# x laid out turned by the host, its norm put on the products, in the input projection of a one-core encoder block

## The chip, the core and the metric

One core of a Trainium2 chip runs the whole block in one launch. The metric is the device time of that launch in microseconds (us). TensorE (PE) multiplies, VectorE (DVE), ScalarE (ACT) and GpSimd (POOL) work on the rest, and transfers are issued on SyncE's queue (SP), on ACT's or on POOL's.

## The reference

The block takes x, 1024 rows of 1024 values in fp32, and computes

```python
h = rms_norm(x, norm1_g[l])
proj = h @ w_in[l]
xr, gr, q, k, v, fl = jnp.split(proj, cuts, axis=-1)
xr = causal_depthwise_conv(xr, conv_w[l], conv_b[l])
y_lru = rg_lru(xr, ...)
y_lru = y_lru * jax.nn.gelu(gr)
log_f = jax.nn.log_sigmoid(fl + fox_bf[l])
y_fox = forgetting_attention(q, k, v, log_f)
x = x + concat(rms_norm(y_lru), rms_norm(y_fox)) @ w_out[l]
x = x + peer(rms_norm(x), ...)
return rms_norm(x, final_g)
```

rms_norm multiplies a row by 1/sqrt(mean of its squares + 1e-6) and each column by a gain. That first factor, one number per row, is called the row root here. Only rms_norm(x, norm1_g) and its product with w_in (1024 x 2568: xr, gr, q, k and v of 512 columns each, fl of 8) are touched by the change. Everything after that product is computed as before.

## The kernel before, in words

The kernel is five stages, one behind the other, each a block of its own that begins when all engines have ended the one before: project (L114), recur (L358), attend (L612), the mixing with w_out, and the expert stages, which hold most of the time. The change is in project and recur.

**The operand.** The product needs h with its columns on the partitions. It lies in m.hh, 8 slices k of 128 columns times 1024 rows, and twice: a high part that ACT rounds and a low part, what is left, that DVE subtracts. The weights of 128 columns of w_in (a chunk i, 20 in all) are split the same way into m.w_hi and m.w_lo. m.w, m.w_hi and m.w_lo hold two chunks each. A product of a chunk for 512 rows (a half) is three terms of 8 matmuls 128x512 (three_terms, L102 to L111): high by high, high by low, low by high. So a product is 24 matmuls.

**project before.** SP loads x in 8 blocks of 128 rows into a ring of four (L164), with the gain on all partitions (L166) and the weights of chunks 0 and 1 (L92). For each block, ACT squares and sums the rows (L214) and takes the root (L216), DVE inverts it (L275) and multiplies row root and gain onto the block (L278, normalize), PE turns the block in 8 transposes (L312, turn), ACT rounds what it reads from PSUM (L208, high) and DVE subtracts (L261, low; one input in PSUM). A product of half 0 needs blocks 0 to 3, one of half 1 all 8. The order is written out by hand: items (L152) begins with chunks 0 and 1 for half 0, then both for half 1, and the last turns lie between and inside the first two products. Then come chunks 2 to 6, the 8 forget columns (L338), and chunk 7. ACT reads every product from PSUM and writes it where it is kept (L247, with gelu for chunks 4 to 7; L242 and L243 for the forget columns). Four PSUM banks hold products in flight. In the same loop ACT rounds the weights of chunk i + 2 (L99) and DVE subtracts (L266). POOL only zeroes tiles and then loads the forget weights, the biases and small constants in a chain of transfers (L180 to L188), each waited for.

**recur before.** It holds 12 chunks, 8 to 19: q, k and v of four pairs of heads. PE multiplies them and in between makes the gates of the recurrence (gates_of, L456 to L465) and turns v (turn_v, L467). ACT reads the products (L495), rounds weights (L99), and makes the sigmoids, tanh, exp and root of one of four channel groups c (L518 to L530). POOL subtracts for the weights' low parts (L443), one 128x1024 operation of two SBUF inputs per chunk, in place of DVE. DVE runs, in order: conv(0), the logarithm of the forget gate, and then for each c fraction(c), conv(c + 1), recurrence(c). PE's gates wait for conv. The sigmoids of c + 1 wait for recurrence(c), because they overwrite r and i (lru_done, L513), and the second pair of gate products of c + 1 needs the two gate banks that those sigmoids read.

## Time and profile before

| what | us |
|---|---|
| three runs, median (lowest to highest) | 2739.32 (2738.11 to 2740.86) |
| profiled execution | 2739.89 |
| its span in the trace | 2738.1 |
| project, from the start to the restart of PE in recur | 0 to 126.8 |
| recur | 126.8 to 279.0 |
| attend, mixing and experts | 279.0 to 2738.1 |

Busy over the span: PE 2669.0 us (97%), DVE 2325.6 (85%), POOL 1443.5 (53%), ACT 1272.2 (46%). A busy share is a mean over stages of very different kinds. For this change one reads the first 280 us by themselves: when PE starts, when it does not run, and what it waits for there.

### The profile page before, as it was taken

The page shows a single profiled execution, that of the slowest core. Times are in us where ns is not written, and L with a number is a line of the kernel's source. Part 1 is how long each engine was busy: PE and PEld are TensorE (multiplying, and loading weights), DVE is VectorE, ACT ScalarE, POOL GpSimd, SP SyncE. Part 2 cuts the span into 40 slices and gives each one's busy share as a digit, 9 for nine tenths or more (in the row PEclk, how much of TensorE's full clock was granted, in tenths as well). Part 3 has the DMA queues.
Part 4 walks back from the last instruction along what each step waited for, and adds up shares of the span by engine and source line. Part 5 has one row for each costly group of instructions (what it writes and reads, how often), then busy time and mean ns, then how long its engine had stood idle before and what let it go on. Part 6 is the DMA issues. An engine that isn't in the chain of part 4 may idle for free. (4 is left out here: it accounts for less than half of the span.)

```text
span 2738.1 us, 40138 instructions
## 1 busy us (share of the span) xinstructions
PE 2669.0 (97%) x14907; PEld 2363.1 (86%) x14907; DVE 2325.6 (85%) x4160; ACT 1272.2 (46%) x2553; POOL 1443.5 (53%) x938
## 2 busy tenths in 40 slices
PE   7999899989999999999999999999999999999998
PEld 6777566679999999999999999997888888888887
DVE  4287897449989999988889898877999999999997
ACT  4244443223332223999898998962222222222222
POOL 2122321024348876666666666654666666666652
PEclk9999899999999999999999999999999999999999
DMA  4110101233248886999999999999999999999995
GB/s 128 39 39 24 62 1 39 77 100 101 62 159 304 304 295 223 376 393 399 398 389 410 402 389 405 394 393 371 388 387 387 387 388 388 388 386 388 388 386 207
DMA packets 333059, 762.67 MB, mean 279 GB/s; under 512 B 24176, under 2 KB 159344, under 8 KB 330304
## 3 DMA queue, kind: packets, MB, share of 16 engines
q0 software_dynamic: 111104, 403.02, 38.8%
q1 hardware_dynamic: 221040, 353.68, 36.1%
q10 hardware_dynamic: 720, 3.41, 0.3%
q8 instruction: 118, 1.93, 0.3%
q14 instruction: 77, 0.63, 0.1%
HBM read 667.73 MB, written 92.27 MB: 278 GB/s over the span
## 5 line engine op out<-in xcount | busy, mean ns | idle before, releaser
L2159 POOL DMA_INDIRECT v_rows<-in_peer_v,row_numbers x336 | 542.0, 1613 | 322.7 <-DVE y_rest L2232 184.7
L1790 PE MATMUL expert_pre<-h2T,wq_then_uT_hi 128*128 128x320 f32 x4096 | 669.3, 312 | 2.3 <-PEq L1469 2.3
L1904 POOL DMA_INDIRECT u_rows<-in_peer_u,row_numbers x384 | 534.9, 1393 | 241.5 <-DVE row_weights L1924 163.3
L1790 PEld LDWEIGHTS expert_pre<-h2T,wq_then_uT_hi 128*128 128x128 f32 x4096 | 609.4, 188 | 2.4 <-issue 2.4
L2289 PE MATMUL expert_out<-v_hi,w_hi 128*128 128x512 f32 x1280 | 500.4, 391 | 11.7 <-DVE w_lo L2210 10.3
L1924 DVE CUSTOM_DVE_ANT_0 u_rows<-u_rows,h_rows_kept 128x1024 f32<-128x1024 f32 x384 | 489.1, 1301 | 23.9 <-DMA u_rows<-in_peer_u,row_numbers 23.6
L2289 PE MATMUL expert_out<-v_lo,w_hi 128*128 128x512 f32 x1280 | 498.8, 390 | 0.0
L2289 PE MATMUL expert_out<-v_hi,w_lo 128*128 128x512 f32 x1280 | 498.7, 390 | 0.0
L1790 PE MATMUL expert_pre<-h2T,wq_then_uT_lo 128*128 128x320 f32 x2048 | 342.0, 309 | 0.0
L2232 DVE SCALAR_TENSOR_TENSOR y_rest<-v_rows,row_weights,y_rest 128x1024 f32<-128x1024 f32 x256 | 326.8, 1280 | 17.9 <-DMA v_rows<-in_peer_v,row_numbers 17.2
L1790 PEld LDWEIGHTS expert_pre<-h2T,wq_then_uT_lo 128*128 128x128 f32 x2048 | 310.9, 188 | 0.0
L2289 PEld LDWEIGHTS expert_out<-v_hi,w_hi 128*128 128x128 f32 x1280 | 240.8, 188 | 66.4 <-DVE w_lo L2210 14.6
L2179 ACT ACTIVATE w_hi<-pick_memory 128x640 fp32r<-128x640 f32 x128 | 94.6, 739 | 436.8 <-DVE pick_memory L2203 436.8
L2289 PEld LDWEIGHTS expert_out<-v_hi,w_lo 128*128 128x128 f32 x1280 | 240.7, 188 | 50.3
L2289 PEld LDWEIGHTS expert_out<-v_lo,w_hi 128*128 128x128 f32 x1280 | 240.9, 188 | 49.6
L1856 ACT ACTIVATE gated_second_hot<-gated_second_hot,routeT,minus_second_and_gate 128x128 f32<-128x128 f32 x640 | 262.9, 485 | 0.2
L2177 ACT ACTIVATE v_hi<-pick_memory 128x1024 fp32r<-128x1024 f32 x128 | 134.9, 1054 | 197.2 <-DMA pick_memory<-in_peer_v 139.3
L1838 ACT ACTIVATE expert_acts<-expert_pre 128x320 f32<-128x320 f32 x256 | 110.0, 430 | 238.0 <-PE expert_pre L1790 237.4
L1848 ACT ACTIVATE gated_second_hot<-iota,minus_second_and_gate 128x128 f32<-128x128 f32 x640 | 203.4, 393 | 0.0
L2216 DVE TENSOR_TENSOR v_lo<-pick_memory,v_hi 128x1024 fp32r<-128x1024 f32 x128 | 156.1, 1219 | 18.2 <-ACT v_hi L2177 18.2
L1778 PE MATMUL spread_ps<-gated_second_hot,first_hot 128*128 128x128 f32 x1280 | 168.3, 274 | 0.0
L110 PE MATMUL product<-hT_hi_lo,w_in_hi 128*128 128x512 f32 x640 | 159.1, 402 | 5.4 <-PEq L158 3.2
(351 smaller groups left out, 3996.2 us busy)
## 6 DMA issues: line engine op xcount, KB each, us to landing
pick_memory<-in_peer_v SPq DMA_DIRECT2D x128, 512.0 KB, 11.7
wq_then_u<-in_peer_u_turned SPq DMA_DIRECT2D x86, 512.0 KB, 8.3
pick_memory<-acts_dram SPq DMA_DIRECT2D x128, 320.0 KB, 11.3
acts_dram<-expert_acts SPq DMA_DIRECT2D x124, 320.0 KB, 6.0
gates_dram<-pick_memory SPq DMA_DIRECT2D x19, 2048.0 KB, 11.1
pick_memory<-gates_dram SPq DMA_DIRECT2D x58, 448.0 KB, 13.0
third_u<-in_peer_u_turned SPq DMA_DIRECT2D x42, 512.0 KB, 8.5
wq_then_u<-in_peer_wq SPq DMA_DIRECT2D x32, 512.0 KB, 3.9
```

The lines of the kernel that those rows point to most:

```text
L110: last = nc.tensor.matmul(to, w[:, i % 2, k], m.hh[:, part, k, cols], start=n == 0, stop=n == len(terms) - 1)
L1778: last = nc.tensor.matmul(spread_ps[:, g % 2, j], first_hot[:, g % SLOTS, j], second[:, g % SLOTS, j], start=True, stop=True)
L1790: last = nc.tensor.matmul(pre[:, (2 * c + half) % 4, 0:WIDTH], part[:, c % 2, k], m.h2T[:, t, k, HALVES[half]], start=n == 0, stop=n == le ...
L1848: last = A(second[:, g % SLOTS, j], m.iota[:], ACT.Abs, bias=minus[:, i % 2, 0, first + j:first + j + 1])
L1856: last = A(second[:, g % SLOTS, j], second[:, g % SLOTS, j], ACT.Relu, scale=minus[:, i % 2, 1, first + j:first + j + 1], bias=routeT[:, i ...
L1904: pool.indirect_dma_start(rows[:, k % RING], None, table, bass.IndirectOffsetOnAxis(ap=m.row_of[:, f, slot:slot + 1], axis=0)).then_inc(fe ...
L1924: v.tensor_tensor_reduce(out=rows[:, k % RING], in0=rows[:, k % RING], in1=m.h2_kept[:, f], scale=1.0, scalar=0.0, op0=ALU.mult, op1=ALU.a ...
L2159: pool.indirect_dma_start(rows[:, k % ROW_RING], None, d.peer_v, bass.IndirectOffsetOnAxis(ap=m.row_of[:, f, slot:slot + 1], axis=0)).then ...
L2177: nc.scalar.activation(vhi[:, n % 2, c], vt[x % V_RING], ACT.Copy).then_inc(vhi_done, 1)
L2216: v.tensor_tensor(vlo[:, n % 2, c], vt[x % V_RING], vhi[:, n % 2, c].bitcast(F32), ALU.subtract).then_inc(vlo_done, 1)
L2232: v.scalar_tensor_tensor(out=m.y_of(f), in0=rows[:, k % ROW_RING], scalar=m.row_weight[:, f, slot:slot + 1], in1=m.y_of(f), op0=ALU.mult, ...
L2289: last = nc.tensor.matmul(out[:, bank], a[:, n % 2, c, tokens], e[:, n % 2, c, cols], start=opens and c == 0 and k == 0, stop=closes and c ...
```

## The change

The host hands in x turned (columns first, x_turned) beside x, and the gain as 128x8. In project, SP loads x_turned in 8 slices k of 128 columns by 1024 rows; all eight have room. The slices are split without the norm: ACT multiplies by the gain while it rounds (high), and DVE makes the low part in one operation from xT and the high part (low, both inputs in SBUF). ACT also squares every slice, and POOL adds the eight squares, 7 additions of 128x1024. PE sums them over the partitions with a matrix of ones (sum_squares, placed behind the fifth product). DVE and ACT make the row root of that, on all partitions (m.root, 128x1024), and it is multiplied onto the products: by DVE in project, as it reads them from PSUM (evict), by POOL in recur, on q, k and v after ACT has stored them, and by DVE on the last v.

PE's first four products (chunks 0 and 1, both halves, four banks) are made slice by slice: three terms of slice k for chunk 0, then for chunk 1, up to k = 3; then slices 4 to 7 for chunk 0, and for chunk 1. The transposes are gone. There are six PSUM banks for products. The first weights come in two parts, the first halves issued by ACT. The forget columns get root and bias in three DVE operations behind the last eviction. In recur, POOL scales 11 chunks, and turn_v waits for that; the convolutions write into parts of xrT that are done with. Between the code that is quoted lie the semaphores' new counts, memory and the host's arrays.

```diff
 def split_high(act, nc, m, i):
-
-    act.wait_ge(m.w_in[i % 2], 16 * (i // 2 + 1))
+    act.wait_ge(m.w_in[i % 2], 16 * (i // 2 + 2))
...
-        items = [(0, 0), (1, 0), (0, 1), (1, 1)] + [(i, half) for i in [*range(2, CHUNKS - 1), FORGET, CHUNKS - 1]
-                                                    for half in range(2)]
+        items = [(i, half) for i in [*range(CHUNKS - 1), FORGET, CHUNKS - 1] for half in range(2)]
...
             def _(sp):
+                def load_x(k):
+                    if k >= X_RING:
+                        sp.wait_ge(x_in[k % X_RING], 16 * (k // X_RING))
+                    sp.dma_start(xT[:, k], d.x_turned[k * P:(k + 1) * P, :]).then_inc(x_in[k % X_RING], 16)
+
+                for k in range(X_RING):
+                    load_x(k)
+                for k in range(X_RING, KT):
+                    if k - X_RING < 2:
+                        sp.wait_ge(m.w_in[k - X_RING], 16)
+                        load_weights(sp, d, m, k - X_RING, PARTS[1])
+                    load_x(k)
...
             def _(pool):
+                for k in range(1, KT):
+                    pool.wait_ge(squared, k + 1)
+                    if k > 1:
+                        pool.wait_ge(zeroed_then_added, BLOCKS + k - 1)
+                    pool.tensor_tensor(square_sum[:], squares[:, 0] if k == 1 else square_sum[:], squares[:, k % SQ_RING],
+                                       ALU.add).then_inc(zeroed_then_added, 1)
                 pool.dma_start(wf[:], d.w_in[:, 5 * G:].rearrange("(k p) n -> p k n", p=P)).then_inc(small_in, 16)
...
+                def high(k):
+                    act.wait_ge(x_in[k % X_RING], 16 * (k // X_RING + 1))
+                    A(m.hh[:, 0, k], xT[:, k], ACT.Copy, scale=gain[:, k:k + 1]).then_inc(high_done, 1)
+
+                def square(k):
+                    if k >= SQ_RING:
+                        act.wait_ge(zeroed_then_added, BLOCKS + max(1, k - SQ_RING))
+                    A(squares[:, k % SQ_RING], xT[:, k], ACT.Square).then_inc(squared, 1)
...
+                act.dma_start(gain[:], d.norm1_turned).then_inc(gain_in, 16)
+                for i in range(2):
+                    load_weights(act, d, m, i, PARTS[0])
...
+                split_part(0, 0)
+                act.wait_ge(gain_in, 16)
+                for k in range(KT):
+                    if k == 1:
+                        split_part(1, 0)
+                    high(k)
+                    if k:
+                        square(k - 1)
+                    if k in (3, 4):
+                        split_part(k - 3, 1)
+                square(KT - 1)
+                for i in range(2):
+                    act.wait_ge(product_done, used(i))
+                    split_high(act, nc, m, i + 2)
+                for half in range(2):
+                    act.wait_ge(mean_made, half + 1)
+                    A(m.root[:, cols_of(half)], m.root[:, cols_of(half)], ACT.Sqrt).then_inc(rooted, 1)
...
+                    if half == 1 and i >= 2:
                         act.wait_ge(product_done, used(i))
                         split_high(act, nc, m, i + 2)
+                    if i >= CT:
+                        act.wait_ge(product_read, reads(n))
+                        gate = m.gateT[:, i - CT, cols_of(half)]
+                        A(gate, gate, ACT.Gelu_apprx_tanh)
...
+                def low(k):
+                    dve.wait_ge(high_done, k + 1)
+                    v.scalar_tensor_tensor(out=m.hh[:, 1, k], in0=xT[:, k], scalar=gain[:, k:k + 1],
+                                           in1=m.hh[:, 0, k].bitcast(F32), op0=ALU.mult, op1=ALU.subtract
+                                           ).then_inc(low_done, 1)
...
+                def evict(n):
+                    i, half = items[n]
+                    dve.wait_ge(product_done, n + 1)
+                    g, c = divmod(i, CT)
+                    to, pad = (m.xrT, d.PAD) if g == 0 else (m.gateT, 0)
+                    v.tensor_tensor(to[:, c, pad + half * HALF:pad + (half + 1) * HALF], product[:, n % BANKS],
+                                    m.root[:, cols_of(half)], ALU.mult).then_inc(product_read, 1)
...
+                split_low(0, PARTS[0], 1)
+                for k in range(KT):
+                    low(k)
+                    if k == 0:
+                        split_low(1, PARTS[0], 2)
+                    if k in (3, 4):
+                        split_low(k - 3, PARTS[1], k)
+                split_low(2)
+                split_low(3)
+                mean(0)
+                mean(1)
+                invert(0)
+                evict(0)
+                invert(1)
...
+                    if half == 1 and i >= 2:
+                        split_low(i + 2)
+                    if i == CHUNKS - 1:
+                        dve.wait_ge(rooted, 2 + half + 1)
+                        part = m.forget[:, cols_of(half)]
+                        own.link(v.tensor_tensor(part, part, forget_more[:, cols_of(half)], ALU.add))
+                        own.link(v.tensor_tensor(part, part, m.root[0:d.FH, cols_of(half)], ALU.mult))
+                        v.tensor_scalar(part, part, fbias[:], None, ALU.add)
...
+                def first_products(i, k):
+                    if k in (0, KT // 2):
+                        pe.wait_ge(m.w_hi_done, i + 1 + (2 if k else 0))
+                    pe.wait_ge(high_done, k + 1)
+                    for term, (w, part) in enumerate(((m.w_hi, 0), (m.w_hi, 1), (m.w_lo, 0))):
+                        if term == 1:
+                            pe.wait_ge(low_done, k + 1)
+                        if term == 2 and k in (0, KT // 2):
+                            pe.wait_ge(m.w_lo_done, i + 1 + (2 if k else 0))
+                        for half in range(2):
+                            end = k == KT - 1 and term == 2
+                            last = nc.tensor.matmul(product[:, 2 * i + half], w[:, i, k], m.hh[:, part, k, cols_of(half)],
+                                                    start=k == 0 and term == 0, stop=end)
...
+                def sum_squares():
+                    pe.wait_ge(zeroed_then_added, BLOCKS + KT - 1)
+                    for half in range(2):
+                        nc.tensor.matmul(sums[:, half], ones[:], square_sum[:, cols_of(half)], start=True, stop=True
+                                         ).then_inc(summed, 1)
+
+                for k in range(KT // 2):
+                    for i in range(2):
+                        first_products(i, k)
+                for i in range(2):
+                    for k in range(KT // 2, KT):
+                        first_products(i, k)
+                for n in range(4, len(items)):
...
+                    if n == 4:
+                        sum_squares()
...
-                for i in range(FIRST + 2, CHUNKS):
-                    pool.wait_ge(m.w_hi_done, i + 1)
-                    pool.tensor_tensor(m.w_lo[:, i % 2], m.w[:, i % 2], m.w_hi[:, i % 2].bitcast(F32), ALU.subtract
-                                       ).then_inc(low_done, 1)
+                for i in range(FIRST, CHUNKS - 1):
+                    pool.wait_ge(product_read, 2 * (i - FIRST) + 2)
+                    p, which = divmod(i - FIRST, 3)
+                    to = (m.q[:, p], m.k[:, p], vT(p))[which]
+                    pool.tensor_tensor(to, to, m.root[:], ALU.mult).then_inc(scaled, 1)
+                    if i + 2 < CHUNKS:
+                        pool.wait_ge(m.w_hi_done, split_count(i + 2))
+                        pool.tensor_tensor(m.w_lo[:, i % 2], m.w[:, i % 2], m.w_hi[:, i % 2].bitcast(F32), ALU.subtract
+                                           ).then_inc(low_done, 1)
+                pool.wait_ge(scaled, CHUNKS - 1 - FIRST)
...
                 def turn_v(p):
-                    pe.wait_ge(product_read, 6 * p + 6)
+                    pe.wait_ge(scaled, 3 * p + 3)
...
                 dve.wait_ge(lru_done, CT)
+                for half in range(2):
+                    n, cols = 2 * (CHUNKS - 1 - FIRST) + half, slice(half * HALF, (half + 1) * HALF)
+                    dve.wait_ge(product_done, n + 1)
+                    v.tensor_tensor(vT(PAIRS - 1)[:, cols], product[:, n % 4], m.root[:, cols], ALU.mult)
...
+        if name == "x":
+            turned = _np.ascontiguousarray(a.T)
```

## Rows read from the trace of the kernel before

**Rows 1.** Busy time by stage: stretch, length, each engine's busy us, clock, DMA.
```profile
0.00:22.08 22.08, 7.85 (x33) 6.28 (x33) 9.90 (x17) 11.73 (x20) 2.23 (x11) 1.00 0.79 261
22.08:39.80 17.72, 16.61 (x81) 13.52 (x81) 13.12 (x19) 9.78 (x19) 5.13 (x7) 1.00 0.31 63
...
124.00:262.00 138.00, 133.66 (x562) 104.55 (x563) 108.89 (x74) 66.41 (x82) 41.08 (x24) 0.99 0.14 39
```

**Rows 2.** Timeline (start, us, engine, line, tiles, idle before), PE's products in project.
```profile
22.08 5.55 PE L110 MATMUL product<-hT_hi_lo,w_in_hi 128*128 128x512 f32 x16 [1.11 <-ACT hT_hi_lo L208]
50.80 3.79 PE L110 MATMUL product<-hT_hi_lo,w_in_hi 128*128 128x512 f32 x16
```

**Rows 3.** Timeline of the first x blocks, and transfers up to 130 us.
```profile
5.83 1.06 ACT L214 ACTIVATE squares<-x_rows 128x1024 f32<-128x1024 f32 x1 [2.31 <-DMA x_rows<-in_x]
...
w_in_columns<-in_w_in SPq DMA_DIRECT2D x12, 512.0 KB, 4.2
```

**Rows 4.** Timeline and groups by shape: the operations that the change multiplies.
```profile
8.35 1.29 DVE L278 SCALAR_TENSOR_TENSOR h_rows<-x_rows,sums,gain 128x1024 f32<-128x1024 f32 x1
...
21.92 1.05 ACT L214 ACTIVATE squares<-x_rows 128x1024 f32<-128x1024 f32 x1
...
L722 POOL TENSOR_TENSOR squares_summed<-squares_summed,squares_T 128x1024 f32<-128x1024 f32 x5 | 11.9, 2376 | 18.0 <-ACT squares_T L890 17.7
```

**Rows 5.** Timeline of DVE and POOL where both have two-input work, mixing and recur.
```profile
140.63 6.54 DVE L78 RECIPROCAL qT<-qT 8x1024 f32<-8x1024 f32 x1
141.36 2.40 POOL L443 TENSOR_TENSOR w_in_lo<-w_in_columns,w_in_hi 128x1024 fp32r<-128x1024 f32 x1 [1.48 <-ACT w_in_hi L99]
165.09 2.28 DVE L601 TENSOR_TENSOR_SCAN forget<-qT 8x1024 f32<-8x1024 f32 x1
166.59 3.62 POOL L443 TENSOR_TENSOR w_in_lo<-w_in_columns,w_in_hi 128x1024 fp32r<-128x1024 f32 x1 [7.72 <-ACT w_in_hi L99]
...
176.56 5.95 DVE L564 SCALAR_TENSOR_TENSOR x_conv<-x_proj_then_attention,conv_taps,x_conv 128x1024 f32<-128x1024 f32 x3
178.36 3.06 POOL L443 TENSOR_TENSOR w_in_lo<-w_in_columns,w_in_hi 128x1024 fp32r<-128x1024 f32 x1 [8.15 <-ACT w_in_hi L99]
236.11 3.93 DVE L564 SCALAR_TENSOR_TENSOR x_conv<-x_proj_then_attention,conv_taps,x_conv 128x1024 f32<-128x1024 f32 x3
...
470.61 2.89 POOL L1094 TENSOR_TENSOR w_out_fox_lo<-w_out_fox_then_x_rows,w_out_fox_hi 128x1024 fp32r<-128x1024 f32 x1 [39.44 <-ACT w_out_fox_hi L1137]
471.21 2.84 DVE L1165 TENSOR_TENSOR fox_columns_lo<-x_proj_then_attention,fox_columns_hi 128x512 fp32r<-128x512 f32 x1
473.45 1.50 POOL L1099 CAST wq_then_uT_hi<-wq_then_u 128x1024 fp32r<-128x1024 f32 x1
481.29 0.69 DVE L1165 TENSOR_TENSOR fox_columns_lo<-x_proj_then_attention,fox_columns_hi 128x512 fp32r<-128x512 f32 x1
```

**Rows 6.** Timeline: project's end and recur's start; a reciprocal (by shape).
```profile
110.42 0.68 DVE L302 TENSOR_TENSOR forget<-forget,forget_of_low_weights 8x512 f32<-8x512 f32 x1 [2.22 <-ACT forget_of_low_weights L243]
...
125.30 1.23 DVE L266 TENSOR_TENSOR w_in_lo<-w_in_columns,w_in_hi 128x1024 fp32r<-128x1024 f32 x1 [10.49 <-ACT w_in_hi L99]
...
126.85 5.50 PE L110 MATMUL product<-hT_hi_lo,w_in_hi 128*128 128x512 f32 x16 [3.17 <-PEq L158]
...
L999 DVE RECIPROCAL inverse_totals<-mixed_values 64x512 f32<-64x512 f32 x16 | 53.7, 3355 | 10.4 <-PE mixed_values L824 10.1
```

**Rows 7.** Timeline of recur: the recurrence, the sigmoids that wait, and PE's gates.
```profile
187.26 1.23 DVE L588 TENSOR_TENSOR gateT<-gateT,i_gate 128x1024 f32<-128x1024 f32 x1
190.47 1.27 ACT L518 ACTIVATE r_gate<-gates,lru_vectors 128x512 f32<-128x512 f32 x2
194.63 1.88 PE L464 MATMUL gates<-x_conv,wx_blocks 128*128 128x512 f32 x4
198.44 0.69 DVE L575 TENSOR_SCALAR x_proj_then_attention<-tanh_m 128x1024 f32<-128x1024 f32 x1 [9.96 <-ACT tanh_m L524]
...
222.01 1.26 ACT L518 ACTIVATE r_gate<-gates,lru_vectors 128x512 f32<-128x512 f32 x2 [5.34 <-DVE gateT L588]
222.75 1.98 PE L464 MATMUL gates<-x_conv,wx_blocks 128*128 128x512 f32 x4 [1.31 <-ACT r_gate L518]
```

More of the change, by code:

```diff
@@ L218, in _ @@
+                for i in range(2):
+                    load_weights(act, d, m, i, PARTS[0])
                 act.wait_ge(m.ident_ready, 2)
                 A(first_root[:], m.ident[:, 0:1], ACT.Sqrt)
-                for b in range(X_RING):
-                    root(b)
-                    if b:
-                        high(b - 1)
-                split_high(act, nc, m, 0)
-                high(X_RING - 1)
-                root(X_RING)
-                split_high(act, nc, m, 1)
-                root(X_RING + 1)
@@ L229, in _ @@
-                high(X_RING)
-                for b in range(X_RING + 2, NT):
-                    root(b)
-                    high(b - 1)
-                high(NT - 1)
+                split_part(0, 0)
[8 more added lines that the diff above has]
+                        split_part(k - 3, 1)
@@ L238, in _ @@
+                A(wf_hi, wf[:], ACT.Copy).then_inc(forget_split, 1)
                 for n, (i, half) in enumerate(items):
-                    act.wait_ge(product_done, n + 1)
                     if i == FORGET:
-                        cols = slice(half * HALF, (half + 1) * HALF)
-                        A(m.forget[:, cols], product[0:d.FH, n % 4], ACT.Identity, bias=fbias[:])
-                        A(forget_more[:, cols], product[LOW:LOW + d.FH, n % 4], ACT.Copy).then_inc(product_read, 1)
+                        act.wait_ge(product_done, n + 1)
+                        A(m.forget[:, cols_of(half)], product[0:d.FH, n % BANKS], ACT.Copy)
+                        A(forget_more[:, cols_of(half)], product[LOW:LOW + d.FH, n % BANKS], ACT.Copy
+                          ).then_inc(rooted, 1)
@@ new lines, in split_low, with mean @@
+                def split_low(i, rows=slice(None), count=None):
+                    dve.wait_ge(m.w_hi_done, count or split_count(i))
+                    v.tensor_tensor(m.w_lo[:, i % 2, rows], m.w[:, i % 2, rows], m.w_hi[:, i % 2, rows].bitcast(F32),
+                                    ALU.subtract).then_inc(m.w_lo_done, 1)
+                def mean(half):
+                    dve.wait_ge(summed, half + 1)
+                    v.tensor_scalar(m.root[:, cols_of(half)], sums[:, half], 1.0 / D, EPS, ALU.mult, ALU.add
+                                    ).then_inc(mean_made, 1)
@@ new lines, in invert @@
+                def invert(half):
+                    dve.wait_ge(rooted, half + 1)
+                    own.link(v.reciprocal(m.root[:, cols_of(half)], m.root[:, cols_of(half)]))
+                def evict(n):
[5 more added lines that the diff above has]
+                                    m.root[:, cols_of(half)], ALU.mult).then_inc(product_read, 1)
@@ L296, in _ @@
-                v.tensor_tensor(wf_lo, wf[:], wf_hi.bitcast(F32), ALU.subtract).then_inc(forget_lo, 1)
-                for i in range(2, CHUNKS + 1):
-                    split_low(i)
-                for half in range(2):
-                    dve.wait_ge(product_read, items.index((FORGET, half)) + 1)
-                    part = m.forget[:, half * HALF:(half + 1) * HALF]
-                    v.tensor_tensor(part, part, forget_more[:, half * HALF:(half + 1) * HALF], ALU.add)
-                split_low(CHUNKS + 1)
+                split_low(0, PARTS[0], 1)
@@ L332, in multiply_forget, with multiply @@
+                def multiply(n):
+                    i, half = items[n]
+                    if half == 0:
+                        pe.wait_ge(m.w_hi_done, split_count(i))
+                        pe.wait_ge(m.w_lo_done, split_count(i))
+                    if n >= BANKS:
+                        pe.wait_ge(product_read, n - BANKS + 1)
+                    three_terms(nc, m, product[:, n % BANKS], i, half).then_inc(product_done, 1)
                 def multiply_forget(n):
-                    cols = slice(items[n][1] * HALF, (items[n][1] + 1) * HALF)
@@ L540, in _ @@
                     for n, (chunk, half) in enumerate((c, h) for c in range(i, i + 3) for h in range(2)):
-                        evict(chunk, half)
+                        if chunk < CHUNKS - 1:
+                            evict(chunk, half)
                         if n == 0 and p:
```

193 lines of the change are left out of this document (69 added, 124 removed).

## The prediction

> **What bounds the kernel now.** I read the busy time by stage first. PE is busy for 7.9 of the first 22.1 us and for 16.6 of the next 17.7; from there to the end of project it has no gap, and in recur it is busy for 133.7 of 138 us [rows 1]. So a saving has to come from the first 40 us, and in the long stretch behind them DVE and ACT are idle most of the time. The timeline of PE comes second. The first product begins at 22.08 and the fifth at 50.80 [rows 2], so the first four end at about 50.7. Two spacings follow: 16 matmuls take 3.6 to 3.8 us at full pace (a product of 24 takes 5.44), and the first 16 took 5.55 [rows 2]. I take the difference, 1.6 us or more, as what PE pays when it starts slow. [...] It pays again at 126.85, behind 3.2 us of idleness, with 5.50 us for 16 [rows 6]. Third, the timeline of DVE and POOL where both have something to do, because the change gives POOL 18 operations of 128x1024 with two SBUF inputs (7 additions, 11 scalings) that it did not have.
>
> **POOL and DVE, the price that decides.** A three-operation run of DVE takes 3.93 us alone and 5.95 us when a POOL subtraction falls into it, and that one takes 3.06 in place of 2.40 [rows 5]. The row pair at 470 us shows who goes first: POOL starts at 470.61 and waits half a us for DVE's operation to end, then DVE's 0.69 us operation takes 2.84, then POOL's copy waits for DVE in turn (1.50 us) [rows 5]. So they alternate, one operation each. A reciprocal is not held (6.54 us, with POOL's 2.40 inside it) [rows 5]. Once POOL waited over two, a scan and the operation behind it (3.62) [rows 5]; that is the only sign against alternation. [...]
>
> **Start of project after.** x slice 0 lands as block 0 does (ACT starts at 5.83 [rows 3]). The half weights come on ACT's queue, which before does not show; 512 KB of them take 4.2 us undisturbed [rows 3], so from 2.6 us on they land at 5.5 at the soonest and about 8 in the crowd. I take 6.8; both ends shift the start by about 1 us. ACT then has 8 highs, 8 squares and 4 half splits, at 1.05 us recorded and 0.95 apart for 1024 elements [rows 4]: high(0) ends at 8.4, high(1) 9.8, squares 0 and 1 by 12.7, high(3) 13.6, high(4) 16.0, high(5) 18.4, high(6) 20.3, high(7) 22.1. ACT never waits for low, and a slice lands before it is wanted. The first addition can start at 12.7. low costs 1.29 (the two-input form [rows 4]), an addition 2.38 [rows 4]. low(0) to low(2) are done by 13.0. From there five lows and two half splits (0.65 each) alternate with seven additions, because squares come each 1.9 to 2.4 us, faster than the pair of operations goes by: low(3) ends at 16.7, low(4) 23.5, low(5) 30.2, low(6) 33.9, the last addition 36.3, low(7) 37.6. The sum is 7 x 2.4 + 5 x 1.29 + 2 x 0.65 = 24.6 behind 13.0.
>
> PE begins at 8.4, is through slices 0 to 3 for both chunks at 20.6 (8 shares of 6 matmuls, 1.36 us each, the start slow), and then waits: for low(4) 2.4 us, low(5) 5.3, low(6) and low(7) each 1 to 3 us, with the pace down. Behind 37.6 come four slow matmuls (1.7 us) and 24 for chunk 1 (5.44 and about 0.8 slow): the fourth product ends at 45.5 where it ended at 50.7. **Gain 5.2.** Unhindered, it would have ended at 31.9 (24 x 4 matmuls in 21.8 us, and the slow start), a gain of 18.8.
>
> **Rest of project.** sum_squares adds two fp32 matmuls to PE's queue. A pair of that form, the gates, takes 1.88 recorded, 1.8 of PE's time [rows 7]: **+1.8**. The root's chain (mean, sqrt, a reciprocal of 512 at 3.36 [rows 6], an eviction of 0.69) is 6 us behind the first sum, and the seventh product, which wants bank 0, comes 6.3 us behind it: 0.5 us to spare, nothing if that holds, up to 1 us if not. Evictions on DVE (16 of 0.69, one SBUF input) and the gelus on ACT lie beside products of 5.44. POOL's chain of constants starts at 36 in place of 22.8 and needs 47 us: it ends near 84, covered by project's end. At the end, DVE's split for chunk 9 (1.23, before at 125.30 [rows 6]) can start 0.5 earlier, since ACT reads no product first; but three forget operations (0.68, 0.68, 0.4 and gaps, [rows 6]) come behind it: **+1.35** until recur starts. The last gelu is covered by them.
>
> **recur.** POOL scales chunk i when ACT has stored it, and then subtracts for chunk i + 2. Its own load is 4.8 us of 10.9 per chunk, up to 9 when DVE holds it: it meets PE's needs, and turn_v's. What counts is DVE. Each scaling costs it 2.0 to 2.3 us unless it meets a reciprocal [rows 5]. By the clock of before, scalings start at 140.3 (beside a reciprocal, free), 154.7, 165.6, 177.3 and 188.2. The second to fourth delay conv(1) by 5.7 us, to 188.1, so PE's first gates wait 0.9 us. The fifth and the subtraction behind it, which before began at 189.24 just behind recurrence(0), both fall into recurrence(0), 4.6 us more: it ends at 198.8, where it ended at 188.5 [rows 7]. The sigmoids of channel group 1 ran at 190.47 and could have run 2.0 earlier for DVE's part; their first half now ends at 199.5, and PE's second gates, at 194.6 before [rows 7], wait for it: 5.1 us with the 0.9, and 1.6 for the slow pace behind the idleness. DVE's idleness at 198.44 (9.96 us [rows 7]) pays the debt off. For group 2 the sigmoids already waited 5.34 us for recurrence(1), and PE 1.31 for them [rows 7]: two more POOL operations meet that recurrence and add 2.1 net. For group 3 the sigmoids come 2.5 us late, and PE's gates, four us behind them in the timeline, do not wait. Sum **+8.5 to +10**; I take 8.5, as the 1.6 may be partly in rows already. The last v on DVE costs 0.1. Bounds: 0 if everything hides, 11 with a second slow start.
>
> **The sum** against the profiled 2739.9: -5.2 + 1.8 + 1.35 + 8.5 = +6.5, so 2746.4; the median of the runs lies 0.6 below that execution, so 2746. All behind recur starts from its end and is taken to shift with it, within 2 us.
>
> **Rivals.** (1) *DVE keeps its turn.* Its operations in project are not linked by waits of its own, and if DVE takes two or three in a row before POOL, as with the scan at 165 [rows 5], low(7) ends by 25 and the fourth product at 32: gain 18 to 18.8, less 3.2 in project; in recur 3 to 8.5 lost. That is 2728 to 2732, I say **2730**, faster; it decides from low(5) ending before 23. Against it: the pair at 470 is the same form (a satisfied wait, then the operation) and POOL got in. Chance 0.2. (2) *Recur absorbs it.* Project as forecast (-2.05), and DVE loses less than 6 us up to the end of recurrence(0): PE then hardly waits, -2.05 + 0 to 2 = **2738 to 2740**. For: several scalings begin within a us of a reciprocal or of DVE idleness, and POOL may slip into it. Chance 0.2. (3) *PE's clock is lost more often*, with an eviction late on top: two more slow starts, 3.2, and 1 to 3 for the seventh product: **2752**. Chance 0.1. That x arrives so late that it sets the pace, so that the slices do nothing, would need a slice landing behind 22; all of x had landed by 22 before, with 0.5 MB more in front. It goes with the forecast.
>
> **How the numbers follow.** Forecast, alternation in both stages: chance 0.5, by itself 2742 to 2751. About 0.2% (5.5 us, 2733.8 to 2744.8) is what can be told from no change. The range 2730 to 2752 takes in rival 1 to its middle and the other two; a tenth is left below, and under a tenth above. Three quarters of the forecast's chance lie above 2744.8. Slower: 0.5 x 0.75 + 0.1 = 0.48. Same: 0.5 x 0.25 + 0.2 = 0.32. Faster: 0.2.
>
> **What would show it.** In the changed kernel's timeline: low(4) to low(7) with recorded durations of 3 us or more, each started before a POOL addition ends, and PE idle for hT_hi_lo between 20 and 38 us; the fifth product at 45 to 46; recur's restart near 124; the sigmoids of group 1 waiting some 8 us for gateT, and PE for them. If lows take 1.3 each and low(7) ends by 25, the alternation is wrong and rival 1 holds. If recur is as long as before (152 us from restart to attend), rival 2.

## The result and the profile after

The changed kernel takes 2746.61 us (median of 8 runs, 2741.65 to 2749.44), the kernel before 2739.70 on the same chip (8 runs). The ratio is 1.0025, with a 95% interval of 1.0016 to 1.0035: slower by a quarter of a percent. The forecast was 2746. Its profiled execution took 2745.85 us, with a span of 2744.1; that of before has a span of 2738.1.

The stages, in us of each profiled span (recur is counted from PE's first product in it to the first transfer of attend):

| | before | after | forecast for after |
|---|---|---|---|
| PE's first product begins | 22.08 | 12.28 | 8.4 |
| fifth product begins | 50.80 | 45.77 | 45.5 |
| recur begins | 126.85 | 124.83 | 124.8 |
| attend begins | 279.04 | 287.49 | 285.5 |
| recur's length | 152.2 | 162.7 | 160.7 |
| end of the span | 2738.1 | 2744.1 | 2744.6 |

The busy time of the changed kernel by stage (stretch, length, busy us of PE, PE's weight loads, DVE, ACT and POOL, the TensorE clock that was granted as a share of the full one, DMA share, GB/s) answers to [rows 1]:

```profile
0.00:45.55 45.55, 25.85 (x96) 19.34 (x97) 27.88 (x14) 20.66 (x23) 26.13 (x23) 0.96 0.46 147
45.55:124.80 79.25, 74.81 (x326) 58.06 (x324) 30.59 (x34) 17.08 (x23) 8.48 (x14) 1.00 0.17 39
124.80:287.50 162.70, 154.59 (x632) 119.52 (x632) 138.95 (x80) 68.44 (x83) 72.85 (x35) 0.96 0.12 33
```

PE does 96 matmuls in the first 45.55 us, 25.9 us of work. In recur DVE's 80 operations take 139 us, and PE's clock is granted at 0.96 where it was 0.99 in [rows 1].

The start of the changed kernel, from its timeline (start, us, engine, line, tiles, idle time before and what ended it); [rows 2] and [rows 3] are its counterparts:

```profile
10.46 0.63 ACT L228 ACTIVATE w_in_hi<-w_in_columns 128x512 fp32r<-128x512 f32 x1 [5.45 <-DMA w_in_columns<-in_w_in]
...
12.28 2.45 PE L350 MATMUL product<-hT_hi_lo,w_in_hi 128*128 128x512 f32 x4 [12.28 <-ACT hT_hi_lo L219]
...
16.71 2.55 POOL L189 TENSOR_TENSOR ares_of_row_by_partition<-squares 128x1024 f32<-128x1024 f32 x1 [13.25 <-ACT squares L224]
...
17.70 2.64 DVE L278 SCALAR_TENSOR_TENSOR hT_hi_lo<-xT,gain,hT_hi_lo 128x1024 fp32r<-128x1024 f32 x1 [0.71 <-ACT hT_hi_lo L219]
...
19.41 18.74 POOL L189 TENSOR_TENSOR ares_of_row_by_partition<-ares_of_row_by_partition,squares 128x1024 f32<-128x1024 f32 x6
...
20.27 2.90 DVE L284 TENSOR_TENSOR w_in_lo<-w_in_columns,w_in_hi 128x512 fp32r<-128x512 f32 x1
...
23.09 3.43 DVE L278 SCALAR_TENSOR_TENSOR hT_hi_lo<-xT,gain,hT_hi_lo 128x1024 fp32r<-128x1024 f32 x1
...
26.45 2.88 DVE L284 TENSOR_TENSOR w_in_lo<-w_in_columns,w_in_hi 128x512 fp32r<-128x512 f32 x1
...
29.25 9.99 DVE L278 SCALAR_TENSOR_TENSOR hT_hi_lo<-xT,gain,hT_hi_lo 128x1024 fp32r<-128x1024 f32 x3
...
32.66 1.22 PE L350 MATMUL product<-hT_hi_lo,w_in_hi 128*128 128x512 f32 x2 [4.43 <-DVE hT_hi_lo L278]
...
39.29 0.73 PE L350 MATMUL product<-hT_hi_lo,w_in_hi 128*128 128x512 f32 x2 [1.65 <-DVE hT_hi_lo L278]
...
45.77 3.79 PE L111 MATMUL product<-hT_hi_lo,w_in_hi 128*128 128x512 f32 x16
```

The reader is to see three things. The half weights, 256 KB a chunk on ACT's queue, are there only at 10.46. From the first addition (16.71) on, seven operations of DVE, five lows and two half splits, take 21.84 us where alone they are 5 of 1.28 and 2 of 0.69, 7.8 in all: DVE is held for 14.0 us, 2.0 for each of the seven additions. And PE waits four times for a low: 0.93, 4.43, 0.38 and 1.65 us, 7.4 in sum.

The middle of recur answers to [rows 7], again from the timeline:

```profile
178.90 2.77 DVE L609 TENSOR_SCALAR x_proj_then_attention<-x_proj_then_attention,conv_taps,lru_vectors 128x1024 f32<-128x1024 f32 x1
...
186.26 2.75 POOL L484 TENSOR_TENSOR kT<-kT,w_root_on_all_partitions 128x1024 f32<-128x1024 f32 x1 [5.14 <-ACT kT L540]
186.80 3.29 DVE L633 TENSOR_TENSOR x_conv<-x_conv,tanh_m 128x1024 f32<-128x1024 f32 x1
188.97 3.37 POOL L487 TENSOR_TENSOR w_in_lo<-w_in_columns,w_in_hi 128x1024 fp32r<-128x1024 f32 x1
190.13 4.37 DVE L634 TENSOR_TENSOR_SCAN i_gate<-r_gate,x_conv 128x1024 f32<-128x1024 f32 x1
194.53 1.23 DVE L636 TENSOR_TENSOR gateT<-gateT,i_gate 128x1024 f32<-128x1024 f32 x1
195.79 1.26 ACT L563 ACTIVATE r_gate<-gates,lru_vectors 128x512 f32<-128x512 f32 x2 [7.36 <-DVE gateT L636]
```

A scaling holds the product in front of the scan (3.29 us), and the subtraction behind it holds the scan (4.37). The first row is of another kind: a tensor_scalar in fp32 with one SBUF input, 2.77 us where the same operation takes 0.81 at 210.70; POOL subtracts beside it, from 177.74 for 3.38 us. recurrence(0) ends 70.9 us behind recur's start; before it ended 61.6 behind it [rows 7]. ACT's sigmoids of group 1, which had waited for nothing, wait 7.36 us, and PE waits for them. PE's own timeline shows the cost, twice:

```profile
196.53 3.65 PE L509 MATMUL gates<-x_proj_then_attention,wx_blocks 128*128 128x512 f32 x4 [3.37 <-ACT r_gate L563]
...
228.46 3.78 PE L509 MATMUL gates<-x_proj_then_attention,wx_blocks 128*128 128x512 f32 x4 [3.38 <-ACT r_gate L563]
231.26 5.55 PE L111 MATMUL product<-hT_hi_lo,w_in_hi 128*128 128x512 f32 x16
```

Each wait is 3.4 us, and each pair of gates behind it takes 3.65 or 3.78 us where it took 1.88 and 1.98 [rows 7]. At 231.26 the next 16 matmuls are slow too, 5.55 us where such a row has 4.2 to 4.5 behind the other gates. The stretch by itself, in the busy times:

```profile
224.83:234.83 10.00, 6.62 (x15) 3.75 (x14) 3.47 (x3) 4.93 (x7) 0.00 (x0) 0.66 0.20 52
```

The mean granted clock is 0.66, so PE spent a part of it at the lower of its two levels, 1.2 GHz for 2.4.

### The profile page after: what moved, and what is told of

The parts are those of the page before. It is cut to its first block and busy times, and to the rows that moved or that the text cites. A ratio compares the mean times of both kernels' runs of the same rounds, so it can differ in the third digit from the quotient of the medians.

```text
span 2744.1 us, 39997 instructions
## 1 busy us (share of the span) xinstructions
PE 2664.7 (97%) x14847; PEld 2356.2 (86%) x14847; DVE 2369.2 (86%) x4164; ACT 1266.9 (46%) x2531; POOL 1487.6 (54%) x957
## 5 line engine op out<-in xcount | busy, mean ns | idle before, releaser
L2341 PE MATMUL expert_out<-v_hi,w_hi 128*128 128x512 f32 x1280 | 500.3, 391 | 10.6 <-DVE w_lo L2262 10.5
L1830 PEld LDWEIGHTS spread_ps<-gated_second_hot,first_hot 128*128 128x128 f32 x1280 | 160.8, 191 | 0.0
```

Of the source, the lines that this page charges most:

```text
L1830: last = nc.tensor.matmul(spread_ps[:, g % 2, j], first_hot[:, g % SLOTS, j], second[:, g % SLOTS, j], start=True, stop=True)
L2341: last = nc.tensor.matmul(out[:, bank], a[:, n % 2, c, tokens], e[:, n % 2, c, cols], start=opens and c == 0 and k == 0, stop=closes and c ...
```

## The experiments

The two places where POOL meets DVE were taken away first, one at a time and both. All ratios are to the kernel before, in runs on the same chip.

**e1_adds8: seven additions of 8 columns.** The sum of squares is right in 8 columns of 1024; the others hold a constant.

```diff
-pool.tensor_tensor(square_sum[:], ..., squares[:, k % SQ_RING], ALU.add)
+few = slice(0, 8)
+pool.tensor_tensor(square_sum[:, few], ..., squares[:, k % SQ_RING, few], ALU.add)
```

> The changed kernel, but POOL's seven additions of the squares are 8 columns wide instead of 1024 (the other 1016 columns of the sum are a constant), so the row root is not that of x; every wait stays. Theory (DVE and POOL exclude each other while both read two SBUF operands): the low parts take 1.3 us each instead of 3.0 to 3.4, the fourth product ends at about 35.6 us instead of 45.6 (31.9 of the unhindered walk plus the 3.7 us by which ACT started late), and the run is about 10 us shorter than the changed kernel, near 2736.6. Rival (ACT's pace or the arrival of x sets PE's waits between 25 and 40 us, the long low parts are only in step with it): the fourth product stays at 45 and the time near 2746.

2738.75 us (10 runs), ratio 0.9995, 0.9985 to 1.0004. The timeline of DVE, POOL and PE:

```profile
20.34 1.28 DVE L279 SCALAR_TENSOR_TENSOR hT_hi_lo<-xT,gain,hT_hi_lo 128x1024 fp32r<-128x1024 f32 x1 [0.35 <-ACT hT_hi_lo L220]
...
26.84 1.29 DVE L279 SCALAR_TENSOR_TENSOR hT_hi_lo<-xT,gain,hT_hi_lo 128x1024 fp32r<-128x1024 f32 x1 [0.71 <-ACT hT_hi_lo L220]
...
36.84 3.79 PE L111 MATMUL product<-hT_hi_lo,w_in_hi 128*128 128x512 f32 x16
```

The lows take 1.28 or 1.29 and end 11.1 us earlier, and the fifth product begins at 36.84 in place of 45.77, recur at 115.9. So the additions cost 8.9 us at this place, and nothing else there held PE. The fifth product is 1.2 us later than I had expected, the time 2.2 above it.

**e2_scale8: scalings of 8 columns.** q, k and v of recur are scaled by the row root in 8 of 1024 rows.

```diff
-pool.tensor_tensor(to, to, m.root[:], ALU.mult).then_inc(scaled, 1)
+pool.tensor_tensor(to[:, 0:8], to[:, 0:8], m.root[:, 0:8], ALU.mult).then_inc(scaled, 1)
```

> The changed kernel, but POOL's eleven scalings of q, k and v are 8 columns wide, so q, k and v keep their values without the row root; every wait stays. Theory (exclusion, read by way of DVE's chain): recurrence(0) ends about 4.6 us earlier relative to recur's start plus 5.7 us of what came before it, PE no longer waits 3.4 us twice for the sigmoids, recur takes 152 to 153 us instead of 162.7, and the run is about 10 us shorter, near 2736.6. Rival (what costs is the changed order of the convolutions, with their buffers in xrT, and their new wait): recur stays within 2 us of 162.7.

2736.54 us (10 runs), ratio 0.9988, 0.9978 to 0.9997. The row of recur in the busy times by stage:

```profile
124.79:276.92 152.13, 149.59 (x632) 117.54 (x632) 120.14 (x80) 68.56 (x83) 47.88 (x35) 0.99 0.13 35
```

Recur is 152.1 us long, as before (152.2). DVE's 80 operations take 120.1 us, 18.8 less than beside the 11 full scalings, 1.7 us for each.

**e3_both8: both edits.**

> Both narrowings at once; the computation left out is that of the two kernels before it. Theory: the two costs are in different stages, so they add: about 20 us shorter than the changed kernel, near 2726, 13 us below the kernel before. Rival (what is saved in front is given back later, since the expert stages are bound by transfers and indirect loads): less than 15 us of the 20 arrive at the end.

2728.11 us (4 runs), ratio 0.9954, 0.9939 to 0.9969. Fifth product at 37.57, recur from 116.64 to 269.42. Of the changed kernel's 2746.6 the additions take 7.9 us, the scalings 10.1, both together 18.5. (The changed kernel was timed beside 2739.7 for the kernel before and these three beside 2740.3, so each may be 0.6 more.) The rest of the change is therefore worth 12 us (2728.1 beside 2740.3 for the kernel before), and the 18 POOL operations eat more than that.

**e4_sum_on_pe: no POOL additions.** The whole computation; ACT writes the squares rounded for TensorE (fp32r), and PE sums them over partitions and slices in 16 matmuls between its first products.

```diff
-for k in range(1, KT): pool.tensor_tensor(square_sum[:], ..., squares[:, k % SQ_RING], ALU.add)
+def sum_squares(k):
+    pe.wait_ge(squared, k + 1)
+    for half in range(2):
+        nc.tensor.matmul(sums[:, half], ones[:], squares[:, k % SQ_RING, cols_of(half)], start=k == 0,
+                         stop=k == KT - 1).then_inc(summed, 1)
```

> Full computation. No additions on POOL: ACT writes the squares rounded for TensorE, and PE sums them slice by slice with 16 matmuls by the ones matrix, accumulated in PSUM, laid between the first products. Theory: as with the narrow additions the low parts are free, at the price of 16 matmuls of 0.227 us (3.6 us) in place of the two fp32 ones (1.8 us): the fifth product begins near 39 us instead of 45.6, and the run is about 8 us shorter than the changed kernel, near 2738.5, so within 0.2% of the kernel before. Rival (ACT's pace): near 2746.

2739.16 us (11 runs), ratio 1.0002, 0.9993 to 1.0011. PE's timeline:

```profile
13.05 2.45 PE L343 MATMUL product<-hT_hi_lo,w_in_hi 128*128 128x512 f32 x4 [13.05 <-ACT hT_hi_lo L212]
...
21.44 0.63 PE L370 MATMUL square_sums_of_rows<-squares,ones_square 128*128 128x512 f32 x2
21.91 1.08 PE L343 MATMUL product<-hT_hi_lo,w_in_hi 128*128 128x512 f32 x4
...
41.65 3.79 PE L111 MATMUL product<-hT_hi_lo,w_in_hi 128*128 128x512 f32 x16
```

PE has no gap from 13.05 on. A pair of summing matmuls takes 0.47 us of its time, eight of them 3.7; with a start 0.65 us later than e1's, that is 4.4 of the 4.8 us by which the fifth product comes later than in e1. I had expected it near 39, 2.65 us earlier: e1's fifth product was itself 1.2 us later than expected, PE started 0.65 later still, and the slow first matmuls took 0.3 more than in e1. The summing I had priced nearly right, at 3.6. Recur begins at 118.91, 5.9 us before after's: 4.1 from the start and 1.8 from the two fp32 matmuls that are gone.

**e5_memset_for_scale: POOL busy, but reading nothing.** In place of each scaling, three fills of m.root, which take 2.98 us. q, k and v of recur stay unscaled.

```diff
-pool.tensor_tensor(to, to, m.root[:], ALU.mult).then_inc(scaled, 1)
+for part in range(3):
+    pool.memset(m.root[:], 1.0).then_inc(scaled, 1)
+    pool.wait_ge(scaled, 3 * (i - FIRST) + part + 1)
```

> The changed kernel, but each of POOL's eleven scalings is three fills of m.root with 1.0 (128x1024, about 0.9 us each, so 2.7 us and nothing read), so q, k and v are not multiplied by the row root; POOL is as busy as with the scalings, its subtractions start as late, and turn_v waits as long. Theory A (what excludes DVE's two-input operations is POOL's reading of SBUF): recur is as short as with the narrow scalings, 152 to 154 us, the run near 2736.6. Theory B (any POOL operation on SBUF holds DVE, as the 5.2 us fill at recur's start holds a tensor_scalar), or what costs is that POOL's low weights and scaled v come late: recur stays at 160 or more and the run near 2745.

2737.93 us (10 runs), ratio 0.9995, 0.9986 to 1.0005. Recur is 152.3 us long. The timeline of POOL and DVE beside one set of fills and the subtraction behind it:

```profile
212.68 2.98 POOL L485 MEMSET w_root_on_all_partitions<- 128x1024 f32 x3 [2.88 <-ACT qT L542]
213.37 1.23 DVE L635 TENSOR_TENSOR x_proj_then_attention<-x_proj_then_attention,tanh_m 128x1024 f32<-128x1024 f32 x1
214.63 2.29 DVE L636 TENSOR_TENSOR_SCAN i_gate<-r_gate,x_proj_then_attention 128x1024 f32<-128x1024 f32 x1
215.74 3.37 POOL L489 TENSOR_TENSOR w_in_lo<-w_in_columns,w_in_hi 128x1024 fp32r<-128x1024 f32 x1
216.95 3.23 DVE L638 TENSOR_TENSOR gateT<-gateT,i_gate 128x1024 f32<-128x1024 f32 x1
```

The product and the scan run at their 1.23 and 2.29 us beside the fills; the subtraction, which reads SBUF, waits for the scan and then holds the next product (3.23). It is POOL's reading that holds DVE's operations of two SBUF inputs, not POOL's being busy, nor the waits and semaphores of the scalings, which are all still there. The Trainium skill (SBUF — State Buffer, "Who interferes with whom") says so too: a DVE instruction with two SBUF inputs contends with a GpSimd instruction that reads SBUF, and not with one that only writes it. This run shows it for such operations alone: the tensor_scalar at recur's start, with one SBUF input, takes 5.72 us here beside POOL's fill of 5.22, where a later one of its size takes 0.82.

**e6_one_queue: the first half weights in SP's queue, each ahead of its x slice.** The whole computation.

```diff
                 for k in range(X_RING):
+                    if k < 2:
+                        load_weights(sp, d, m, k, PARTS[0])
                     load_x(k)
...
-                for i in range(2):
-                    load_weights(act, d, m, i, PARTS[0])
```

> Full computation. The changed kernel, but SP issues the first halves of the two weight chunks in front of x slices 0 and 1; ACT's queue carries the gain alone. Theory: the weights, in 512-byte rows on a queue of their own, landed behind 2 MB of x in 4096-byte rows (10.46 us, 8 us after their issue); in one queue they land at 6 to 7, ACT's first high part ends near 8.5 instead of 12.1, the low parts' alternation with POOL begins 3.5 us earlier, and the run is 3 us shorter than the changed kernel, near 2743.5. Rival (the alternation or the sum has slack at its front): no difference, 2746.5.

2743.14 us (11 runs), ratio 1.0015, 1.0006 to 1.0024. The timeline of ACT and PE:

```profile
5.19 0.63 ACT L230 ACTIVATE w_in_hi<-w_in_columns 128x512 fp32r<-128x512 f32 x1 [1.19 <-DMA w_in_columns<-in_w_in]
...
6.57 1.15 ACT L221 ACTIVATE hT_hi_lo<-xT,gain 128x1024 fp32r<-128x1024 f32 x1 [0.75 <-DMA xT<-in_x_turned]
...
7.86 2.45 PE L350 MATMUL product<-hT_hi_lo,w_in_hi 128*128 128x512 f32 x4 [7.86 <-ACT hT_hi_lo L221]
```

The first weights are there at 5.2 in place of 10.5, PE begins 4.4 us earlier, and the fifth product and recur 3.1 us earlier. Recur stays as long as in the changed kernel, 162.4 us. So the late weights were worth 3.1 us, which the slice-wise start had lost.

**e7_evict_on_dve: e4, and in recur DVE reads q, k and v from PSUM with the root, in place of ACT and POOL.** The whole computation; 24 evictions of 0.69 us stand at fixed places of DVE's order.

```diff
+def evict(n):
+    dve.wait_ge(product_done, n + 1)
...
+    v.tensor_tensor(to, product[:, n % 4], m.root[:, cols], ALU.mult).then_inc(product_read, 1)
...
+behind_link = {4: 0, 18: 1, 20: 2, 26: 3, 30: 4, 34: 5, 36: 6, 38: 7, 40: 8, ...}
+behind_group = {0: (9, 10), 1: (14,), 2: (18, 19), 3: (22, 23)}
```

> Full computation. The kernel with the squares summed on PE, and in recur no scalings on POOL: DVE reads q, k and v from PSUM and multiplies by the row root there (24 operations of 128x512, one SBUF input, 0.69 us), laid by hand between its other operations; ACT reads no products in recur. Theory: 22 more DVE operations of 0.65 us cost it 14.5 us of recur's 152 but are held by nobody and fit where it waited; recur takes 152 to 155 us, the run is 8 to 10 us shorter than with the sum on PE alone (2739.2), near 2730. Rival (DVE becomes late for its own chain, or a bank is free too late, since an eviction waits behind a 6.55 us reciprocal): recur stays above 158, the run at 2736 or more.

2736.21 us (11 runs), ratio 0.9993, 0.9984 to 1.0002. Recur begins at 118.4 and lasts 155.7 us, 0.7 above what I expected and 3.5 more than before. An eviction on DVE takes 0.69 us, and none is held. The time is 6 us above what I expected and the one that the rival gave, though recur stays below the rival's 158. Against the changed kernel recur begins 6.4 us earlier and is 7.0 shorter, but the stages behind it take 2.5 us more (below).

**e8_all: e7, e6, and the three forget operations once, ahead of the last eviction.** The whole computation.

> Full computation. The kernel before in this list, with the weights' first halves in SP's queue in front of x, and the forget columns' three operations done once for both halves in front of the last eviction of project. Theory: 3.5 us from the start, 1.5 to 1.9 from project's end: near 2725, 0.5% below the kernel before. Rival (with the low parts free, the start no longer sets the first products' end, or later stages do not shift): 2728 to 2730.

2732.68 us (8 runs), ratio 0.9975, 0.9964 to 0.9985: faster than both kernels. The time lies above both the 2725 that I expected and the rival's 2728 to 2730. The start did its part: fifth product at 36.11, recur from 111.61, 6.8 us earlier than in e7. But recur took 157.9 us, 2.2 more than there, and the stages behind it 2.1 more (below). PE's waits in it and just before it (engine and line, what was waited for, us in total, times, longest):

```profile
PE turned_v L508 <- DVE kT L598: 2.8, 1, 2.8
PE gates L500 <- ACT r_gate L547: 2.7, 2, 1.4
PE product L111 <- PEq L159: 2.7, 1, 2.7
PE gates L500 <- DVE x_proj_then_attention L622: 1.3, 1, 1.3
```

The first row is one eviction of v that stands behind four operations of the forget chain.

**e9_late_evictions: e8 with another order of DVE's evictions.** The whole computation.

```diff
-behind_link = {4: 0, 18: 1, 20: 2, 26: 3, 30: 4, 34: 5, 36: 6, 38: 7, 40: 8, 44: 11, 45: 12, 48: 13,
+behind_link = {4: 0, 18: 1, 20: 2, 26: 3, 30: 4, 31: 5, 36: 6, 44: 11,
-behind_group = {0: (9, 10), 1: (14,), 2: (18, 19), 3: (22, 23)}
+behind_group = {0: (7, 8, 9, 10), 1: (12, 13, 14), 2: (18, 19), 3: (22, 23)}
```

> The whole computation, with the edits of e8_all; only the order of DVE's evictions in recur is another. In e8_all recur took 158.0 us, and PE waited in it for DVE four times: 2.77 us ahead of the first turning of v, for the eviction of the last half of v (DVE had it behind four operations of the forget chain), 1.41 and 1.30 us ahead of the second gate products of groups 1 and 2, and 1.30 us for conv(2). Here that half of v is evicted three operations earlier, and four evictions of 0.69 us that stood ahead of the ends of recurrence(0) and recurrence(1) stand behind them, where DVE was idle 3.5 and 4.1 us. Theory one, that these waits are what makes e8_all's recur longer than the kernel before's 152.2: the 2.77 us go, the other three shrink by the 1.3 us each that the moved evictions took, recur is 152 to 154 us, and the time is 2726 to 2729. Theory two, that an earlier start of recur is given back whatever DVE does (by PE's granted clock, or by a wait that comes last next): recur stays at 156 or more, and the time at 2731 to 2733. Behind recur the earlier runs differ by up to 2.4 us in attend and by up to 3.6 us in the expert stages with the same instructions, so that up to 3 us of the gain may be lost there; the length of recur tells the theories apart, not the time.

2726.66 us (5 runs), ratio 0.9959, 0.9945 to 0.9972, the fastest of all that keep the whole computation. Recur, which was to tell the two theories apart, lasts 155.5 us, between the 152 to 154 of one and the 156 of the other. The same rows of PE's waits:

```profile
PE product L111 <- PEq L159: 2.7, 1, 2.7
PE gates L500 <- ACT r_gate L547: 2.6, 2, 1.3
PE gates L500 <- DVE x_proj_then_attention L622: 1.8, 2, 1.0
```

The wait for v is gone, and with it 2.5 us of recur. The waits for the gates are not: four evictions that I moved away had not been their cause, or a chain beside DVE's came last in their place; which of the two stays open. Of the 7.3 us between the spans of e8 and e9, recur gives only 2.5. The medians are 6.0 us apart, and 5.0 when each is taken against the kernel before on its own chip (2739.32 and 2738.29).

**What lies behind recur.** The rest is in the stages that no kernel here changes. From the first transfer of attend to the end:

| kernel | attend begins | from there to the end | of it attend |
|---|---|---|---|
| before | 279.04 | 2459.1 | 187.6 |
| after | 287.49 | 2456.6 | 186.2 |
| e1 | 277.09 | 2459.4 | 188.3 |
| e2 | 276.92 | 2457.6 | 186.3 |
| e3 | 269.42 | 2460.7 | 187.2 |
| e4 | 280.35 | 2456.5 | 186.3 |
| e5 | 277.30 | 2456.7 | 186.9 |
| e6 | 284.09 | 2456.4 | 186.2 |
| e7 | 274.06 | 2459.1 | 187.6 |
| e8 | 269.54 | 2461.2 | 187.9 |
| e9 | 267.01 | 2456.4 | 186.4 |

They differ by 4.8 us with the same instructions. The busy time of attend's first 40 us, before, after and in e8:

```profile
279.04:319.04 40.00, 32.95 (x122) 22.81 (x122) 33.89 (x62) 20.43 (x30) 17.69 (x16) 0.79 0.27 106
```

```profile
287.49:327.49 40.00, 32.57 (x125) 22.35 (x126) 35.02 (x62) 21.40 (x32) 18.70 (x16) 0.83 0.28 106
```

```profile
269.54:309.54 40.00, 32.76 (x119) 22.37 (x120) 34.05 (x61) 20.52 (x30) 17.67 (x16) 0.74 0.28 105
```

The granted clock is 0.79, 0.83 and 0.74 there, and after has done 3 matmuls more than before and 6 more than e8; from there to 2585 the mean of all three is 1.00. The last stretch of e8 shows the same, 0.98 and 584 matmuls in the 145 us that end 0.7 us before its span does, beside 0.99 and 600 in the same stretch before:

```profile
2585.00:2730.00 145.00, 134.39 (x584) 110.11 (x582) 123.79 (x140) 38.80 (x55) 63.50 (x41) 0.98 0.81 297
```

```profile
2592.40:2737.40 145.00, 136.22 (x600) 112.15 (x598) 126.68 (x142) 39.33 (x55) 64.49 (x43) 0.99 0.82 303
```

It does not follow attend's start in any plain way (e1 and e5 begin 0.2 us apart and differ by 2.7), and what decides it was not tried. The runs of one kernel scatter by as much: 2737.6 to 2745.2 for e4. Each row is one execution; e3's is the slowest of its four (3.9 us above their median), e9's the fastest of its five (1.4 below), so part of these differences is such scatter and not the kernel's.

## Why the prediction held, step by step

The time was right, 2746 for 2746.6, and so was its reason. Two of the steps inside were wrong, though, and cancelled each other, and two were off in size. That it came out within 1 us is in part luck: recur took 2.0 us more than forecast, and the stages behind it gave back 2.5.

- **The price that decides.** Right. POOL and DVE alternate one for one, the additions held DVE for 14.0 us, and e1, e2 and e5 show that nothing else does it: without the additions every low takes 1.3, without the scalings' reads recur is as long as before.
- **Half weights at 6.8.** Wrong. They landed at 10.46, outside my "about 8 in the crowd": PE began 3.9 us late, at 12.28, and the first addition at 16.71 in place of 12.7. The step that failed is the bound: I priced the transfer by the 4.2 us of [rows 3] and let the crowd put its landing off to 8 at the latest, but it took 8.1 us from its issue. That row is a median of twelve loads, ten of which lie behind 20 us. The kernel before's first 20 us by themselves, where the first two loads share the queue with x, have the warning that I had not looked for:

```profile
w_in_columns<-in_w_in SPq DMA_DIRECT2D x2, 512.0 KB, 9.6
```

- **Seven additions, 24.6 us.** Too high by 2.4, counted from the first addition (24.9 forecast from there, 22.5 measured). The first addition held DVE for 1.36 us, as low(3) came 1.0 us into it, and the other six for 2.05 to 2.21 each, where I had put 2.4 for each of seven. low(7) ended at 39.24 instead of 37.6: only 1.6 of the late start were left.
- **The slow pace behind low(7), 1.6 us.** It did not come: PE's last wait was 1.65 us, and from 39.29 on its 28 matmuls took 6.5 us to the start of the fifth product, which is full pace. That gave back nearly all of the 1.6: the fifth product began at 45.77, and the fourth was forecast to end at 45.5. The gain, 5.0 for the 5.2 forecast, is right by errors that cancel, which is luck.
- **sum_squares, +1.8.** Right: the fifth and the seventh product begin 12.65 us apart with it between them, and two products take 10.88. The root's chain had 0.6 us to spare (0.5 forecast), and the seventh product did not wait.
- **Project's end, +1.35.** Right: PE stood still for 4.47 us ahead of recur, 1.30 more than before, and recur began 2.02 us earlier, forecast 2.05.
- **recur, +8.5.** The mechanism and its place are right, the size was 2 us short; +10.5 lies in the bounds of 0 to 11. recurrence(0) came 9.3 us late (10.3 forecast), PE's second gates waited 3.37 us (5.1 forecast with a wait of the first gates, which did not come), and those of group 2 waited 3.38 where they had waited 1.31, which is the 2.1 net I gave them. The mis-sized term is the pace: I priced one slow start at 1.6 and took part of it off again; there were two, of some 1.8 and 2.7 us by the starts of PE's rows beside those of before. PE's idle time rose by 5.7 us, and its busy time for the same 632 matmuls by 4.8, from 149.8 to 154.6.
- **Everything behind shifts, within 2 us.** It gave back 2.5. That is why the end came at +6.0 with recur at +10.5 and project at -2.0.

Of the rivals, the first (DVE keeps its turn, 2730) was right in price: e3, where the hold is taken away, takes 2728.1. Its mechanism did not decide: in project no operation of DVE took two turns in a row while POOL had one waiting. In recur it happened as in [rows 5], with the same scan and the operation behind it (POOL's subtraction took 5.04 us there), and changed nothing. The second is refuted by recur's length, 162.7 and not 152 to 154. The third's two slow starts did come, but both inside recur.

## What to carry to other kernels

Before work is moved to GpSimd because it is idle, count the VectorE operations with two SBUF inputs that run beside it: each full-size GpSimd operation that reads SBUF cost VectorE 1.7 to 2.0 us here on average, so 18 of them ate 18.5 us and turned a gain of 12 into a loss of 7. Count its fp32 tensor_scalar operations too, which were held beside such operations (2.77 us for 0.81). If the moved work reads PSUM on VectorE (0.69 us each, in every one of 24), or is summed by TensorE (0.47 us for a pair of matmuls, in place of a GpSimd addition of 2.4), nothing is held. Two waits of TensorE of 3.4 us cost 5.1 and 6.1 us with the pace behind them, so it pays to place each side operation behind the one for which TensorE waits.

## What the hardware showed that I had not expected

- **A transfer of short rows beside one of long rows.** 256 KB of weights in rows of 512 bytes on ACT's queue, beside x in rows of 4 KB on SP's, took 8.1 us to land; the same 256 KB took 3.2 us (issued at 2.03, in use at 5.19) at the head of SP's own queue. From the list of transfers of the changed kernel (KB each, median us to landing):

```profile
xT<-in_x_turned SPq DMA_DIRECT2D x8, 512.0 KB, 5.3
w_in_columns<-in_w_in SPq DMA_DIRECT2D x4, 512.0 KB, 3.8
w_in_columns<-in_w_in ACTq DMA_DIRECT2D x2, 256.0 KB, 8.1
```

  The Trainium skill (DMA: Bandwidth & Descriptors, "Queues, rings and completion order") says that each engine takes turns between queues by the packet. By it, as an estimate, the queue with the smaller packets gets the smaller share, and in the first 30 us of the changed kernel ACT's queue moved 0.53 MB in 1200 packets of the profile, SP's 5.24 MB in 3248. But no run here parts this from other causes: x was also issued first, and the full weights of the kernel before, in x's own queue, took 9.6 us.
- **TensorE's pace behind a wait.** Behind 1.65 us of waiting PE went on at full pace; behind 3.37 and 3.38 it ran its next pair of gates at about half, and behind 4.43, at 32.66, its next three pairs took 1.22, 1.05 and 1.05 us where such a pair takes 0.62.
- **ACT's copy with a scale per partition** takes 1.13 us for 128x1024, its square 1.05.
- **A pair of fp32r matmuls 128x512** takes 0.63 us recorded, a pair of fp32 ones of four recorded instructions 1.88.
